# Expert weights in rows of four runs, and turns moved from TensorE to VectorE

## The chip, the cores and the metric

One NeuronCore of a Trainium2 chip runs the whole program. The time is the device time of one execution in microseconds (us). The engines are TensorE (PE in the profile, its weight loads PEld), VectorE (DVE), ScalarE (ACT), GpSimd (POOL) and SyncE (SP). SP issues all the transfers here, and the core has 16 DMA engines that carry them.

## The reference, cut to what matters

The program is a small network of two blocks over 256 context and 256 latent tokens of 1024 features, all in float32. The change touches two places of it. The first is a mixture of eight experts over the 256 latent tokens, of which each token uses two:

```python
D_MODEL = 1024
D_FF = 2816
N_EXPERTS = 8
TOP_K = 2

def _swiglu(h, w1, w3, w2):
    return (jax.nn.silu(h @ w1) * (h @ w3)) @ w2
```

`w1` and `w3` of an expert are 1024 x 2816 and `w2` is 2816 x 1024, so that an expert has 3 x 1024 x 2816 x 4 bytes = 34.6 MB of weights and the eight together have 276.8 MB. A token's outputs of its two experts are weighted by its gates and summed. The second place is an attention with two softmaxes per head, subtracted from each other, over four heads and 256 latent queries.

## The kernel before, in words

Every engine has its own instruction stream, and semaphores order them. The program runs through its stages one after the other; weights come through ring buffers in SBUF.

**The expert stage.** A router on the chip gives each expert the places of its tokens. Each of the eight experts is one block of work (more blocks would follow if an expert had more than 96 tokens). A block works on 96 token slots in three groups (`g`) of 32. The loop over blocks is the same on TensorE, VectorE, ScalarE and SP; `pe_moe`, `ve_moe` and `ac_moe` count each engine's steps in it.

- **Gather.** A selection matrix `pm` (tokens x slots, ones and zeros) picks the expert's tokens out of `atok`. TensorE multiplies it (`gather`, L1282), and ScalarE copies the result to `ac_` (L1868), with the features on the partitions. This is done for the next block while a block still runs.
- **Up.** The 2816 hidden features are cut into two halves `p` of 1408, and each half into four parts of 352. For a half, TensorE goes over eight feature tiles `k` of 128; for each it takes one item of `w1` and one of `w3`. A matmul has 32 slots of `ac_` as its stationary side and 352 columns of an item as its moving side, and four of them stand side by side in the array's columns and write four quarters of the partitions (L1337).
- **Gated values.** ScalarE takes silu of one product (L1889), VectorE multiplies it by the other into `hid` (L2638). A row of `hid` is a slot, and slots of part `t` lie on partitions 32t to 32t+31.
- **Turn.** The down product needs the hidden features on the partitions. TensorE turns `hid` in pieces of 128, 128 and 96 columns (`hidden_turned`, L1321), ScalarE copies the pieces to `gT` (L1894, L1895).
- **Down.** 24 items of `w2` follow, for each part two of 128 rows and one of 96; each takes 12 matmuls of 256 columns (L1359). The outputs are copied by ScalarE (L1904), and brought back to the tokens with the gates by `outputs_back` (L1293); VectorE adds them to `h` (L2611).

**Its transfers.** A block has 56 items (`ITEMS`): 32 of `w1` and `w3` (128 rows of 1408 numbers, 704 KB) and 24 of `w2` (512 or 384 KB). They go through 14 slots (`MRING`). SP issues item i when TensorE has used the item that was in its slot before (L584), so up to 14 items are under way or waiting. A source is 128 rows (or 96) that follow each other in the matrix, row on partition:

```python
src = src[one, k * P:k * P + P, n0:n0 + MCOLS]
...
src = src.rearrange("e p n -> p (e n)")
sy.dma_start(dst, src).then_inc(m_full[i % MRING], 16)
```

**The attention with two softmaxes** has eight units `w_`. For each, TensorE makes scores (`scores2`, L1453), VectorE finds the maxima (`maxima2`, L2685), ScalarE takes exponents, VectorE combines the two (L2693 to L2696), TensorE turns the weights (`weights_turned2`, its instructions are at L737), ScalarE copies them, and TensorE multiplies by the values (`values2`, L1472). Scores of unit w+1 are issued ahead of the turn of unit w. They use banks 0 and 1 or 2 and 3 in turn.

Of the kernel before, what the change touches and what calls it, by code (L numbers as in the profile page):

```python
# [21 lines left out]
ACT = mybir.ActivationFunctionType  # L22
# [224 lines left out]
def build(nc, w, out, counts, stop="end"):  # L247
# [5 lines left out]
    with ExitStack() as ctx:  # L253
# [169 lines left out]
        ac_ = cut(arena, 0, KT, CAP)  # L423
        hid = cut(arena, 768, 2, GROUPS_OF, PART)
        gT = cut(arena, 2880, 2, GROUPS_OF, 3 * P)
# [7 lines left out]
        TURN_BANKS = ((4, 5, 4), (4, 0, 1))  # L433
# [41 lines left out]
        def _(sy):  # L475
# [49 lines left out]
            while s < len(slots):  # L525
# [45 lines left out]
                if s == first["moe"]:  # L571
# [7 lines left out]
                    def block_in(e, expert):  # L579

                        one = bass.ds(expert, 1)
                        for i in range(ITEMS):
                            prev = (i - MRING) % ITEMS
# [12 lines left out]
                            src = src.rearrange("e p n -> p (e n)")  # L596
# [24 lines left out]
        def _(pe):  # L621
# [680 lines left out]
            def expert_block(e, mark):  # L1302
# [9 lines left out]

                def landed(i):
                    pe.wait_ge(m_full[i % MRING], e * (16 * (ITEMS // MRING)) + 16 * (i // MRING + 1))
                    return m_slots[i % MRING]

                def hidden_turned(p, g):

                    b = bank[TURN_BANKS[p][g]]
                    for o, n in PIECES:  # L1320
                        i = nc.tensor.transpose(b[0:n, o:o + P], hid[:, p, g, o:o + n], ident)  # L1321
                    i.then_inc(pe_moe, mark(PEM, ("turned", p, g)))

                for p in range(2):
                    for k in range(KT):
                        ws = [landed(16 * p + 2 * k + i) for i in range(2)]
                        for g in range(GROUPS_OF):
                            if k == 0 and p == 0 and g == 0:
                                of_act_last("gathered")
# [4 lines left out]
                            for i_ in range(2):  # L1334
                                b = bank[UP_BANKS[p][2 * g + i_]]
                                for t in range(4):
                                    i = mm(b[32 * t:32 * t + 32, 0:PART], ac_[:, k, 32 * g:32 * g + 32],  # L1337
# [12 lines left out]
                for n, (p, t, piece) in enumerate(BLOCKS_AT):  # L1350
                    o, rows_ = PIECES[piece]
                    ws = landed(32 + n)
                    for g in range(GROUPS_OF):
                        if n == 0:
                            of_vec(("hid", 1, 0))
                        if n % 12 == 0:
                            of_act(("gT", p, g))
                        for q in range(4):
                            i = mm(bank[Y_BANKS[g]][32 * q:32 * q + 32, 0:256],  # L1359
                                   gT[0:rows_, p, g, o + 32 * t:o + 32 * t + 32],  # L1360
                                   ws[0:rows_, 256 * q:256 * q + 256], start=(n == 0),
                                   stop=(n == len(BLOCKS_AT) - 1), skip_group_check=True)
                    i.then_inc(pe_moe, mark(PEM, ("down", n)))
                    if n in (1, 2, 3):
                        of_vec(("hid", 1, n - 1))
                        if n == 1:
                            of_act(("gT", 0, 2))
                        hidden_turned(1, n - 1)
                    if n == 7:
                        of_vec(("hid", 1, 2))  # L1370
                        of_act(("gT", 1, 2))
# [25 lines left out]
            pe.wait_ge(ac_moe, blocks * aper + aper)  # L1397
            outputs_back().then_inc(pe_done, did(PE, "back last"))
# [162 lines left out]
        def _(ac):  # L1561
# [303 lines left out]
            def gathered(name, inc, counter):  # L1865

                for h in range(2):
                    act(ac_[:, 4 * h:4 * h + 4, :], cut(bank[4 - 4 * h], 0, 4, CAP), ACT.Copy  # L1868
                        ).then_inc(inc, did(counter, name if h else (name, 0)))

            ac.wait_ge(pe_done, at(PE, "gather first"))
            gathered("gathered first", act_done, AC)
# [5 lines left out]
            with ac.Fori(0, blocks) as e:  # L1878
# [4 lines left out]
                for p in range(2):  # L1883
# [7 lines left out]
                    for g in range(GROUPS_OF):  # L1891
                        of_pe(("turned", p, g))
                        b = bank[TURN_BANKS[p][g]]
# [922 lines left out]
```

## Time and profile before

| | |
|---|---|
| median of 3 runs | 3294.95 us (3294.92 to 3304.92) |
| the profiled execution | 3293.41 us, span 3291.6 us |
| TensorE busy | 3116.3 us, 95% of the span |
| VectorE busy | 1283.0 us, 39% |
| ScalarE busy | 588.3 us, 18% |
| granted clock of TensorE, mean | 0.972 |
| expert stage, first to last of its up and down matmuls | 1657.6 to 2455.6 us |

Each matmul in float32 stands in the profile as two records. Busy time of TensorE counts its records' modelled spans; where it is busy without a gap, the starts of records tell how fast it goes. The DMA share is the mean busy share of the 16 DMA engines; it can read a little over 1.

### The profile page before, as it was taken

What the parts mean: (1) busy time and instruction counts of PE and PEld (TensorE: products, weight loads), DVE (VectorE), ACT (ScalarE), POOL (GpSimd) and SP (SyncE); (2) the same over time, 40 slices, a digit from 0 to 9 for tenths busy, and PEclk for the clock granted to TensorE, in tenths of its full rate; (3) what the DMA queues carried; (4) which work ended last, traced back from release to release, by engine and by line L of the source; (5) the groups of instructions that cost most, each with busy time, mean ns of one, the idle gap of its engine ahead of it and who ended that gap; (6) DMA issues with size and microseconds to landing.
All of it is one profiled execution on the core that took longest, in us unless ns stands there. A gap on an engine that the chain in (4) does not pass through costs nothing.

```text
span 3291.6 us, 52527 instructions
## 1 busy us (share of the span) xinstructions
PE 3116.3 (95%) x22488; PEld 2069.7 (63%) x22488; DVE 1283.0 (39%) x2836; ACT 588.3 (18%) x1314; POOL 0.2 (0%) x4
## 2 busy tenths in 40 slices
PE   7999899999999999999999999999999879988998
PEld 5454799997344443457745555445557568876887
DVE  1568666666799887503410101000112232122211
ACT  2114222222211111203310110010111220012000
POOL 0000000000000000000000000000000000000000
PEclk8999999999999999999999999999999889999999
DMA  7241001001577886330189999999984114531452
GB/s 264 75 154 51 1 1 40 1 1 39 189 239 243 245 248 187 123 99 25 70 317 362 357 339 337 343 362 367 349 231 130 51 52 141 153 115 51 133 148 64
DMA packets 351595, 551.15 MB, mean 167 GB/s; under 512 B 14512, under 2 KB 292400, under 8 KB 348048
## 3 DMA queue, kind: packets, MB, share of 16 engines
q1 hardware_dynamic: 351376, 547.89, 50.2%
q8 instruction: 178, 2.92, 0.4%
q14 instruction: 41, 0.34, 0.0%
HBM read 546.80 MB, written 1.05 MB: 166 GB/s over the span
## 4 chain that ended last, share of the span: by engine, by line
PE 89%; DVE 6%; ACT 2%; DMA 2%; issue 1%; SPq 0%; DVEq 0%; ACTq 0%
PE bank L666 15%; PE bank L1337 14%; PE bank L928 9%; PE bank L1130 8%; PE bank L1359 8%; PE bank L1517 7%; PE bank L1144 3%; PE bank L631 3%; PE bank L745 3%; PE bank L1171 2%; PE bank L1075 2%; DVE mix L2079 2%; PE bank L912 1%; PE bank L1282 1%; DMA arena<-in_ada_w 1%; PE bank L1426 1%
## 5 line engine op out<-in xcount | busy, mean ns | idle before, releaser
L666 PE MATMUL bank<-a,ring 128*128 128x256 f32 (+1 forms) x1792 | 454.8, 417 | 19.0 <-ACT a L1614 12.0
L666 PEld LDWEIGHTS bank<-a,ring 128*128 128x128 f32 x1792 | 344.9, 193 | 126.5 <-issue 74.5
L2079 DVE SCALAR_TENSOR_TENSOR mix<-arena,csil,mix 128x256 f32<-128x256 f32 x1008 | 402.0, 476 | 45.6 <-ACT mix L1618 45.6
L1337 PE MATMUL bank<-ring,arena 128*32 128x352 f32 x5376 | 406.9, 461 | 2.7 <-ACT small L1876 2.7
L1337 PEld LDWEIGHTS bank<-ring,arena 128*32 128x32 f32 x5376 | 175.1, 110 | 221.4 <-issue 220.4
L1130 PE MATMUL bank<-a,ring 128*128 128x512 f32 x704 | 307.5, 596 | 6.8 <-ACT a L1614 6.8
L1130 PEld LDWEIGHTS bank<-a,ring 128*128 128x128 f32 x704 | 133.2, 191 | 179.7 <-issue 178.0
L1517 PE MATMUL bank<-arena,ring 128*128 128x256 f32 x1024 | 223.5, 379 | 1.9 <-DVE arena L2736 1.9
L1618 ACT ACTIVATE arena<-bank 128x256 f32<-128x256 f32 (+1 forms) x303 | 142.0, 473 | 451.7 <-PE bank L928 199.2
L2638 DVE TENSOR_TENSOR arena<-arena,bank 128x352 f32<-128x352 f32 x48 | 25.0, 521 | 501.3 <-ACT arena L1889 501.3
L1359 PE MATMUL bank<-ring,arena 128*32 128x256 f32 (+1 forms) x3840 | 219.0, 380 | 0.6 <-issue 0.6
L1517 PEld LDWEIGHTS bank<-arena,ring 128*128 128x128 f32 x1024 | 194.4, 190 | 29.1 <-DVE arena L2736 2.8
L928 PE MATMUL bank<-arena 128*128 128x128 f32 x1408 | 180.6, 281 | 3.1 <-DVE arena L2344 2.1
L928 PEld LDWEIGHTS bank<-arena 128*128 128x128 f32 x1408 | 166.4, 193 | 14.6 <-ACT arena L1618 6.7
L1359 PEld LDWEIGHTS bank<-ring,arena 128*32 128x32 f32 (+1 forms) x3840 | 121.9, 110 | 83.5 <-issue 9.5
L1144 PE MATMUL bank<-arena,ring 128*128 128x512 f32 x352 | 154.1, 597 | 2.1 <-DVE arena L2460 2.1
L2717 DVE TENSOR_SCALAR tmpA<-bank,mods 128x256 f32<-128x256 f32 x32 | 15.5, 484 | 288.4 <-PE bank L1517 213.9
L1144 PEld LDWEIGHTS bank<-arena,ring 128*128 128x128 f32 x352 | 67.5, 192 | 88.4 <-issue 85.5
L1567 ACT ACTIVATE mix<-a 128x256 f32<-128x256 f32 x64 | 21.8, 417 | 534.1 <-DVE a L1994 534.1
L1618 ACT ACTIVATE mix<-arena,csil 128x256 f32<-128x256 f32 x144 | 64.7, 499 | 261.6 <-DMA arena<-in_ada_w 160.6
L745 PE MATMUL bank<-a,ring 128*128 128x512 f32 (+1 forms) x224 | 99.1, 596 | 0.0
L2732 DVE TENSOR_SCALAR tmpA<-bank 128x256 f32<-128x256 f32 x64 | 27.2, 424 | 167.1 <-PE bank L666 167.1
(411 smaller groups left out, 3360.6 us busy)
## 6 DMA issues: line engine op xcount, KB each, us to landing
ring<-in_moe_w SPq DMA_DIRECT2D x224, 704.0 KB, 8.4
ring<-in_mlp_w SPq DMA_DIRECT2D x64, 1024.0 KB, 5.5
ring<-in_moe_w SPq DMA_DIRECT2D x112, 512.0 KB, 8.4
arena<-in_ada_w SPq DMA_DIRECT2D x96, 512.0 KB, 3.8
arena<-in_w_ada SPq DMA_DIRECT2D x48, 512.0 KB, 3.6
ring<-in_ffn_w SPq DMA_DIRECT2D x22, 1024.0 KB, 8.5
arena<-in_moe_w SPq DMA_DIRECT2D x32, 704.0 KB, 8.8
ring<-in_moe_w SPq DMA_DIRECT2D x48, 384.0 KB, 8.4
```

Of the source, the lines that this page charges most:

```text
L631: i = mm(bank[b][:, 0:tile.shape[-1]], const("mean"), tile, start=(k == 0), stop=(k == KT - 1))
L666: i = mm(bank[b][:, 0:n], ws[:, k, t * P:t * P + P], rhs[:, k, sl], start=(k == 0), stop=(k == KT - 1))
L745: i = mm(bank[RKV_BANK[n]][0:m, :], ws[:, k, n % 2 * P:n % 2 * P + m], aT[:, k, :], start=(k == 0), stop=(k == KT - 1), skip_group_check=True)
L928: i = mm(bank[b][:, o + P * m:o + P * m + P], lhs[:, m, :], rhs[:, m, :], start=True, stop=True, skip_group_check=True)
L1075: i = mm(bank[MIX_BANKS[j % 5]], ws[:, k, j % 2 * P:j % 2 * P + P], src, start=(k == 4), stop=(k == 3), skip_group_check=True)
L1130: i = mm(bank[2 * t + i_], ws[:, k, t * P:t * P + P], aT[:, k, :], start=(k == 0), stop=(k == KT - 1))
L1144: i = mm(bank[2 + n % 4], ws[:, k, :], G[:, k, :], start=(k == 0), stop=(k == FT - 1))
L1337: i = mm(b[32 * t:32 * t + 32, 0:PART], ac_[:, k, 32 * g:32 * g + 32], ws[i_][:, PART * t:PART * t + PART], start=(k == 0), stop=(k == KT ...
L1359: i = mm(bank[Y_BANKS[g]][32 * q:32 * q + 32, 0:256], gT[0:rows_, p, g, o + 32 * t:o + 32 * t + 32], ws[0:rows_, 256 * q:256 * q + 256], s ...
L1517: j = mm(bank[4 + n % 2][:, 0:TL], ws[:, k, :], G2[:, 16 * half + k, :], start=(half + k == 0), stop=(half * k == 15))
L1618: act(dst, src, ACT.Copy, scale=scale).then_inc(act_done, did(AC, name))
L2079: ins = V.scalar_tensor_tensor(dst, x, cond, dst, ALU.mult, ALU.add)
```

## The change

It has three parts.

1. **Rows of the weight items.** An item is now made of four runs of 32 rows. For `w1` and `w3` run t begins at row 256t + 32k; for `w2` at row 352t + 32c of the half (`DOWN`, c from 0 to 10). `w2` has 22 items of 128 rows, a block has 54 items. The constants `PIECES`, `BLOCKS_AT` and `TURN_BANKS` go.
2. **Turns.** `gather` now has 32 columns of the selection as its stationary side in four column tiles and 256 columns of tokens as its moving side. VectorE's 32 x 32 block transpose turns its result from PSUM into `ac_` (3 per block, 128 x 256), and turns each `hid` into `gT` in SBUF (6 per block, 128 x 352). TensorE's `hidden_turned` and ScalarE's copies of both go.
3. **Scores.** `scores2` runs two units ahead in place of one.

```diff
-PIECES = ((0, 128), (128, 128), (256, 96))
-BLOCKS_AT = [(p, t, i) for p in range(2) for t in range(4) for i in range(3)]
-ITEMS = 32 + len(BLOCKS_AT)
+DOWN = [(p, c) for p in range(2) for c in range(PART // 32)]
+ITEMS = 32 + len(DOWN)
...
                             if i < 32:
                                 k, n0 = i % 16 // 2, MCOLS * (i // 16)
-                                src = w["moe_w3" if i % 2 else "moe_w1"][0]
-                                src = src[one, k * P:k * P + P, n0:n0 + MCOLS]
+                                src = w["moe_w3" if i % 2 else "moe_w1"][0][one, :, n0:n0 + MCOLS]
+                                src = src.rearrange("e (t r) n -> (e t) r n", t=4)[:, 32 * k:32 * k + 32, :]
                             else:
-                                p, t, piece = BLOCKS_AT[i - 32]
-                                o, n = PIECES[piece]
-                                f0 = MCOLS * p + PART * t + o
-                                src = w["moe_w2"][0][one, f0:f0 + n, :]
-                                dst = dst[0:n, 0:D]
-                            src = src.rearrange("e p n -> p (e n)")
+                                p, c = DOWN[i - 32]
+                                src = w["moe_w2"][0][one, MCOLS * p:MCOLS * p + MCOLS, :]
+                                src = src.rearrange("e (t r) n -> (e t) r n", t=4)[:, 32 * c:32 * c + 32, :]
+                                dst = dst[:, 0:D]
                             sy.dma_start(dst, src).then_inc(m_full[i % MRING], 16)
...
-                for f in range(KT):
+                for g in range(GROUPS_OF):
                     for c in range(2):
-                        i = mm(bank[0 if f >= 4 else 4][:, (f % 4) * CAP:(f % 4) * CAP + CAP],
-                               atok[:, c, f * P:f * P + P], pm[:, c, :], start=(c == 0), stop=(c == 1),
-                               skip_group_check=True)
+                        for q in range(4):
+                            i = mm(bank[4 * (g // 2)][32 * q:32 * q + 32, 256 * (g % 2):256 * (g % 2) + 256],
+                                   pm[:, c, 32 * g:32 * g + 32], atok[:, c, 256 * q:256 * q + 256],
+                                   start=(c == 0), stop=(c == 1), skip_group_check=True)
...
                             if k == 0 and p == 0 and g == 0:
-                                of_act_last("gathered")
+                                of_vec_last(("gathered", GROUPS_OF - 1))
+                                of_act_last("gates")
...
-                        if p == 1 and k in (2, 3, 4):
-                            if k == 2:
-                                of_vec(("hid", 0, 2))
-                            if k == 4:
-                                of_act(("gT", 0, 0))
-                            hidden_turned(0, k - 2)
...
-                        if n == 0:
+                        if n == 0 and g == 0:
+                            of_vec(("gT", 0, 2))
                             of_vec(("hid", 1, 0))
-                        if n % 12 == 0:
-                            of_act(("gT", p, g))
+                        if c == 0 and p == 1:
+                            of_vec(("gT", 1, g))
...
             scores2(0)
+            scores2(1)
             for w_ in range(len(DIFF_UNITS)):
-                if w_ + 1 < len(DIFF_UNITS):
-                    scores2(w_ + 1)
+                if w_ + 2 < len(DIFF_UNITS):
+                    scores2(w_ + 2)
                 weights_turned2(w_)
...
+            def gathered(g, inc, counter, name):
+                V.transpose(ac_[:, g, :], bank[4 * (g // 2)][:, 256 * (g % 2):256 * (g % 2) + 256]
+                            ).then_inc(inc, did(counter, (name, g)))
...
+                def hidden_turned(p, g):
+
+                    ve.wait_ge(ve_moe, e * per + at(VEM, ("hid", p, g)))
+                    V.transpose(gT[:, p, g, :], hid[:, p, g, :]).then_inc(ve_moe, did(VEM, ("gT", p, g)))
```

**SP, the transfers of `w2` in a block.** The last two numbers or three are the shape of the side in SBUF. Before, at the start of the down items:

```order
L597 DMA ring<-in_moe_w 128x1024
L597 DMA ring<-in_moe_w 96x1024
L597 DMA ring<-in_moe_w 128x1024
L597 DMA ring<-in_moe_w 128x1024
L597 DMA arena<-in_moe_w 96x1024
```

and in the changed kernel:

```order
L598 DMA ring<-in_moe_w 128x1x1024
L598 DMA ring<-in_moe_w 128x1x1024
L598 DMA ring<-in_moe_w 128x1x1024
L598 DMA ring<-in_moe_w 128x1x1024
L598 DMA arena<-in_moe_w 128x1x1024
```

The 96-row transfers are gone, and each side has three dimensions now: 128 x 1 x 1024 in SBUF against 4 x 32 x 1024 in the source, as the slicing in the diff leaves it. The transfers of `w1` and `w3` change from 128x1408 to 128x1x1408 (source 4 x 32 x 1408) in the same way.

**TensorE, the second half of a block.** Before (here one row stands for both records of a matmul), from the middle of the second up half to the end of the down product:

```order
L1337 MATMUL bank<-arena 32x352 x24
L1337 MATMUL bank<-ring,arena 32x352 x48
L1359 MATMUL bank<-ring,arena 32x256 x24
L1321 MATMUL bank<-consts,arena 128x128 x2
L1321 MATMUL bank<-consts,arena 96x128
L1359 MATMUL bank<-ring,arena 32x256 x12
L1321 MATMUL bank<-consts,arena 128x128 x2
L1321 MATMUL bank<-consts,arena 96x128
L1359 MATMUL bank<-ring,arena 32x256 x12
```

and now, up to the next block's up product (L1336 is the up product, L1352 the down product, L1284 the gather):

```order
L1336 MATMUL bank<-ring,arena 32x352 x48
L1352 MATMUL bank<-ring,arena 32x256 x96
L1295 MATMUL bank<-arena 128x256 x24
L1352 MATMUL bank<-arena 32x256 x24
L1352 MATMUL bank<-ring,arena 32x256 x60
L1366 MATMUL bank<-consts,arena 128x128 x6
L1352 MATMUL bank<-ring,arena 32x256 x24
L1284 MATMUL bank<-arena 32x256 x24
L1352 MATMUL bank<-ring,arena 32x256 x60
```

The turns between the products are gone, the gather has 24 matmuls of 256 columns in place of 16 of 96, and the down product has 264 matmuls in place of 288.

**TensorE, the attention with two softmaxes.** Before, its first units:

```order
L1453 MATMUL bank<-arena 128x512 x4
L737 MATMUL bank<-consts,arena 128x128 x4
L1453 MATMUL bank<-arena 128x512 x2
L737 MATMUL bank<-consts,arena 128x128 x4
L1472 MATMUL bank<-arena 128x128 x4
L1453 MATMUL bank<-arena 128x512 x2
```

and now:

```order
L1441 MATMUL bank<-arena 128x512 x6
L738 MATMUL bank<-consts,arena 128x128 x4
L1441 MATMUL bank<-arena 128x512 x2
L738 MATMUL bank<-consts,arena 128x128 x4
L1460 MATMUL bank<-arena 128x128 x4
L1441 MATMUL bank<-arena 128x512 x2
```

The order around each unit is the same, but the scores that stand ahead of a turn are those of one unit later.

## Rows read from the trace of the kernel before

**Rows 1.** The page of the profile: the span and the engines' busy time.
```profile
span 3291.6 us, 52527 instructions
PE 3116.3 (95%) x22488; PEld 2069.7 (63%) x22488; DVE 1283.0 (39%) x2836; ACT 588.3 (18%) x1314; POOL 0.2 (0%) x4
```

**Rows 2.** Waits, 1650 to 2470 us: who waited for whom, total, times, longest.
```profile
PE bank L1337 <- ACT small L1876: 2.7, 1, 2.7
...
PE bank L1359 <- issue: 0.6, 1, 0.6
```

**Rows 3.** Waits of SP's queue in the same stretch.
```profile
SPq L597 <- PE bank L1337: 351.8, 128, 22.3
SPq L597 <- PE bank L1359: 196.3, 172, 4.6
```

**Rows 4.** Windows: the third expert's block as a whole.
```profile
core 0: us, PE busy (x) PEld busy (x) DVE busy (x) ACT busy (x) POOL busy (x), PEclk, DMA share, GB/s
1857.92:1957.28 99.36, 99.36 (x1452) 51.33 (x1448) 8.40 (x22) 10.02 (x26) 0.00 (x0) 1.00 1.01 352
```

**Rows 5.** Timeline of TensorE in the second block: start, us, instructions.
```profile
1758.56 21.49 PE L1337 MATMUL bank<-ring,arena 128*32 128x352 f32 x288
...
1797.73 0.55 PE L1321 MATMUL bank<-consts,arena 128*128 128x128 f32 x3
1798.21 3.76 PE L1337 MATMUL bank<-ring,arena 128*32 128x352 f32 x48
...
1845.09 3.81 PE L1282 MATMUL bank<-arena 128*128 128x96 f32 x32
1848.83 6.69 PE L1359 MATMUL bank<-ring,arena 96*32 96x256 f32 x120
1855.33 2.77 PE L1359 MATMUL bank<-arena 128*32 128x256 f32 x48
```

**Rows 6.** Windows of the second block, while `w1` and `w3` load.
```profile
1763.00:1770.00 7.00, 7.00 (x100) 3.14 (x96) 0.00 (x0) 0.00 (x0) 0.00 (x0) 1.00 1.01 418
1770.00:1780.00 10.00, 10.00 (x140) 4.45 (x136) 0.00 (x0) 0.00 (x0) 0.00 (x0) 1.00 1.02 414
1790.00:1800.00 10.00, 10.00 (x135) 4.30 (x131) 0.00 (x0) 0.54 (x2) 0.00 (x0) 1.00 1.02 409
```

**Rows 7.** Windows of the last block, while `w2` loads.
```profile
2398.70:2406.70 8.00, 8.00 (x107) 3.43 (x111) 0.00 (x0) 1.09 (x4) 0.00 (x0) 1.00 1.02 229
...
2414.70:2422.70 8.00, 8.00 (x131) 4.29 (x125) 0.09 (x1) 1.63 (x6) 0.00 (x0) 1.00 1.04 250
2422.70:2430.70 8.00, 8.00 (x148) 5.29 (x141) 1.99 (x6) 0.00 (x0) 0.00 (x0) 1.00 1.03 267
```

**Rows 8.** Timeline of SP: the first expert items issued.
```profile
1630.48 6.42 SPq L597 DMA_DIRECT2D ring<-in_moe_w  x12
```

**Rows 9.** The page's transfers by line: count, KB each, median us to landing.
```profile
ring<-in_moe_w SPq DMA_DIRECT2D x224, 704.0 KB, 8.4
```

**Rows 10.** The chain that ended last: the last down matmuls.
```profile
2446.32 9.26 PE bank L1359 x168
```

**Rows 11.** Timeline of TensorE in the attention with two softmaxes, one unit.
```profile
2610.40 1.12 PE L737 MATMUL bank<-consts,arena 128*128 128x128 f32 x4 [2.50 <-DVE arena L2696]
2611.31 1.92 PE L1472 MATMUL bank<-arena 128*128 128x128 f32 x8
2613.16 1.13 PE L1453 MATMUL bank<-arena 64*128 64x512 f32 x4
2616.79 1.11 PE L737 MATMUL bank<-consts,arena 128*128 128x128 f32 x4 [2.51 <-DVE arena L2696]
```

**Rows 12.** Timeline of VectorE in the same unit.
```profile
2614.34 1.29 DVE L2685 TENSOR_REDUCE small<-bank 128x1 f32<-128x512 f32 x2 [3.99 <-PE bank L1453]
...
2615.99 0.75 DVE L2696 SCALAR_TENSOR_TENSOR arena<-arena,small 128x512 f32<-128x512 f32 x1
```

**Rows 13.** Groups of instructions in the third block: the nearest VectorE row.
```profile
L2638 DVE TENSOR_TENSOR arena<-arena,bank 128x352 f32<-128x352 f32 x6 | 3.1, 521 | 63.7 <-ACT arena L1889 63.7
```

More of the change, by code:

```diff
@@ L53, with uses @@
 MRING, MCOLS, PART = 14, 1408, 352
-PIECES = ((0, 128), (128, 128), (256, 96))
-BLOCKS_AT = [(p, t, i) for p in range(2) for t in range(4) for i in range(3)]
-ITEMS = 32 + len(BLOCKS_AT)
+DOWN = [(p, c) for p in range(2) for c in range(PART // 32)]
+ITEMS = 32 + len(DOWN)
+def uses(i):
+    return len(range(i % MRING, ITEMS, MRING))
 RING = 6
@@ L420, in build @@
         NA_UNITS = [(j, qt) for j in range(KT) for qt in range(2)]
-        ac_ = cut(arena, 0, KT, CAP)
+        ac_ = cut(arena, 0, GROUPS_OF, 256)
         hid = cut(arena, 768, 2, GROUPS_OF, PART)
-        gT = cut(arena, 2880, 2, GROUPS_OF, 3 * P)
+        gT = cut(arena, 2880, 2, GROUPS_OF, PART)
         yp, pgt = cut(arena, 5184, GROUPS_OF, 256), cut(arena, 5952, GROUPS_OF, 256)
@@ L582, in block_in @@
                         for i in range(ITEMS):
-                            prev = (i - MRING) % ITEMS
+                            prev = i - MRING if i >= MRING else i + MRING * (uses(i) - 1)
                             sy.wait_ge(pe_moe, e * per + (at(PEM, taken(prev)) - (per if i < MRING else 0)))
@@ L1311, in of_vec, with of_vec_last @@
                     pe.wait_ge(ve_moe, e * vper + at(VEM, name))
+                def of_vec_last(name):
+                    pe.wait_ge(ve_moe, e * vper + (at(VEM, name) - vper))
                 def landed(i):
-                    pe.wait_ge(m_full[i % MRING], e * (16 * (ITEMS // MRING)) + 16 * (i // MRING + 1))
+                    pe.wait_ge(m_full[i % MRING], e * (16 * uses(i)) + 16 * (i // MRING + 1))
                     return m_slots[i % MRING]
[L1317 to L1322, printed above, removed]
                 for p in range(2):
@@ L1343, in expert_block @@
                             i.then_inc(pe_moe, mark(PEM, ("up", p, k)))
[L1344 to L1351 removed]
+                for n, (p, c) in enumerate(DOWN):
                     ws = landed(32 + n)
                     for g in range(GROUPS_OF):
[L1354 removed]
+                        if n == 0 and g == 0:
+                            of_vec(("gT", 0, 2))
                             of_vec(("hid", 1, 0))
[L1356 to L1357 removed]
+                        if c == 0 and p == 1:
+                            of_vec(("gT", 1, g))
                         for q in range(4):
                             i = mm(bank[Y_BANKS[g]][32 * q:32 * q + 32, 0:256],
[L1360 to L1362 removed]
+                                   gT[:, p, g, 32 * c:32 * c + 32],
+                                   ws[:, 256 * q:256 * q + 256], start=(n == 0),
+                                   stop=(n == len(DOWN) - 1), skip_group_check=True)
                     i.then_inc(pe_moe, mark(PEM, ("down", n)))
[L1364 to L1368, printed above, removed]
                     if n == 7:
                         of_vec(("hid", 1, 2))
[L1371 removed]
                         of_act_last(("y", 2))
@@ L1397, in _ @@
             pe.wait_ge(ac_moe, blocks * aper + aper)
+            pe.wait_ge(ve_moe, blocks * vper + vper)
             outputs_back().then_inc(pe_done, did(PE, "back last"))
@@ L1863, in _ @@
             pper, vper = at(PEM, ("per", "moe")), at(VEM, ("per", "moe"))
[L1865 to L1872, printed above, removed]
             ac.wait_ge(act_done, now(AC))
@@ L1890, in _ @@
                             ).then_inc(ac_moe, did(ACM, ("sg", p, g)))
-                    for g in range(GROUPS_OF):
-                        of_pe(("turned", p, g))
-                        b = bank[TURN_BANKS[p][g]]
-                        act(gT[:, p, g, 0:256], b[:, 0:256], ACT.Copy).then_inc(ac_moe, did(ACM, ("gT part", p, g)))
-                        act(gT[0:96, p, g, 256:384], b[0:96, 256:384], ACT.Copy
-                            ).then_inc(ac_moe, did(ACM, ("gT", p, g)))
                 of_pe("gates turned")
@@ L1899, in _ @@
                 act(pgt[:, 2, :], bank[2][:, 0:256], ACT.Copy).then_inc(ac_moe, did(ACM, "gates"))
-                of_pe("gather")
-                gathered("gathered", ac_moe, ACM)
-                of_pe(("down", len(BLOCKS_AT) - 1))
+                of_pe(("down", len(DOWN) - 1))
                 for g in range(GROUPS_OF):
@@ L2604, in _ @@
             pper, aper = at(PEM, ("per", "moe")), at(ACM, ("per", "moe"))
+            def gathered(g, inc, counter, name):
+                V.transpose(ac_[:, g, :], bank[4 * (g // 2)][:, 256 * (g % 2):256 * (g % 2) + 256]
+                            ).then_inc(inc, did(counter, (name, g)))
             ve.wait_ge(pe_done, at(PE, "gather first"))
+            for g in range(GROUPS_OF):
+                gathered(g, vec_done, VE, "gathered first")
+            ve.wait_ge(vec_done, now(VE))
             counts.count[VEM] = per
@@ L2640, in _ @@
                                         ).then_inc(ve_moe, did(VEM, ("hid", p, g)))
+                        if g:
+                            hidden_turned(p, g - 1)
+                    hidden_turned(p, GROUPS_OF - 1)
                 of_pe("back")
@@ L2643, in _ @@
                     back_added(f, ve_moe, VEM, "h")
+                of_pe("gather")
+                for g in range(GROUPS_OF):
+                    gathered(g, ve_moe, VEM, "gathered")
                 ve.wait_ge(ve_moe, e * per + now(VEM))
```

3 lines of the change are left out of this document (1 added, 2 removed).

## The prediction

> **What bounds the kernel now.** I read the page first: TensorE is busy for 95% of the span [rows 1], so the question for every stage is whether TensorE is what ends it. For the expert stage the windows answer it. A block takes 99.36 us and TensorE is busy for all of them, at the full clock of 1.00, which is 2.4 GHz [rows 4]. In the list of waits TensorE waited in the whole stage once for ScalarE, 2.7 us, and never for a transfer [rows 2]; SP, on the other hand, waited for TensorE 128 and 172 times, 351.8 and 196.3 us [rows 3]. So TensorE bounds the stage, and the transfers follow it.
>
> The reader is to see in the same row that the margin behind it is thin: 34.6 MB in 99.36 us are 348 GB/s, the row shows 352, and the 16 DMA engines' share reads 1.01 [rows 4]. While `w1` and `w3` load, at a share of 1.01 to 1.02, they move 409 to 418 GB/s [rows 6]; I take 415, which is 26 GB/s for each of the 16 engines. While `w2` loads in the last block the share is as full (1.02 to 1.04), but they move only 229 to 267 [rows 7], about 244, or 15.3 GB/s for each. A row of an item is some kilobytes long in both (5.6 and 4.1); what differs is that a third of the `w2` items have 96 rows. How the rows of an item are dealt to the engines thus decides the rate. That is the point at which this change must be judged.
>
> **What it takes from TensorE.** Per block:
> - six turns go. One takes from 1797.73 to 1798.21 [rows 5], 0.48 us: 2.88 us.
> - 24 down items become 22. A record goes by every 54.2 ns (1848.83 to 1855.33 for 120) [rows 5], an item has 12 matmuls or 24 records: 48 records are 2.60 us.
> - the gather takes from 1845.09 to 1848.83 now [rows 5], 3.74 us. Its 24 new matmuls have the shape of the down product, so 48 x 54.2 ns = 2.60 us: 1.14 us less.
>
> That is 6.62 us of 99.36, and 53 us over eight blocks, if TensorE stays the bound.
>
> **What VectorE gets.** Nine transposes per block that the trace of before does not show. The nearest row is the gating product of the same 128 x 352, 0.52 us [rows 13]. From nothing to four times that, one costs 0 to 2.1 us; I take 0.5, and 4.5 us per block beside 8.40 busy of 99 [rows 4]. What waits for them: the up product of the next block waits for the last gathered turn, which may start when the gather ends and has five down items of 1.30 us = 6.5 us of cover, and three turns fit even at 2.1 us. The down product's second half waits for the second half's turns with eleven items of cover, 14 us. So they cost nothing in the block; if the cover were gone they would cost up to 6 us per block. Ahead of the first block the three turns stand on the way once: +1.5 us, against some 1 us that the first gather saves. ScalarE's copies that go were not waited for.
>
> **The attention.** A unit takes from 2610.40 to 2616.79 [rows 11], 6.4 us, and TensorE waits 2.5 us of it for VectorE's combined weights; VectorE in turn waited 3.99 us for the scores [rows 12]. With scores two units ahead, the maxima (1.29) and the combination (about 1.1 with its two small instructions) follow each other without TensorE between, 2.4 us per unit, and TensorE's own work of 1.12 + 1.92 + 1.13 = about 4.1 us becomes the bound. Seven periods shrink by some 2.3 us: -16 us. If the order of waits gives nothing: 0.
>
> **What it does to the transfers.** An item's source was 128 rows in one dimension, and is now 4 runs of 32 rows; its side in SBUF is still 128 rows. Packets keep their length. What may change is the dealing. In the trace of before every large transfer has 128 or 96 rows as its outermost dimension on both sides, and the share shows that all 16 engines work. If an item is dealt by the outermost dimension, 4 on the one side and 128 on the other leave four equal portions, and four engines carry everything while twelve stand idle.
>
> The Trainium skill, "DMA: Bandwidth & Descriptors", section "Why a DMA increments its semaphore by 16 and not by 1", states just this: the number of engines is the largest up to 16 that divides the slowest dimension of both access patterns, and the lowest-numbered ones are taken. By that rule this item runs on four. No row of before can show it, as none has such a shape.
>
> I take four engines as the likeliest case. The price: 276.8 MB at 4 x 26 = 104 GB/s are 2662 us; at 4 x 15.3 = 61 GB/s 4538 us. Four runs of 32 neighbouring rows are less even over SBUF than a 128-row item dealt over sixteen engines, but whole, so I stay near the upper rate and take 25 GB/s per engine, 100 in all: 2768 us, or 346 us per block. TensorE's work in a block, 92.7 us, lies beside that, even at the lower of its clocks (185 us).
>
> **The sum.** The first item is issued at 1630.48 [rows 8] and moves 1 us later: 1631.5. The last lands 2768 + 2 us later; TensorE's last down item is 1.3 us: 4402.8. Before, the last down matmul ended at 2446.32 + 9.26 = 2455.58 [rows 10], and 3291.6 - 2455.58 = 836.0 us of span followed it [rows 1, 10]; less 16 for the attention: 5222.8. Around the span lay 3293.41 - 3291.6 = 1.8 us, and the median of the runs lies 1.5 us over the profiled one: **5226 us**, 1.59 times before. I say 5230.
>
> **The rivals.**
> - **Four engines that get in each other's way (31%).** Engines now walk partitions 0, 32, 64 and 96 upwards together, and if two of them need one entry to SBUF at a time, they share its rate. For it: the 244 GB/s at a full share [rows 7], which show that a dealing can cost 40% of the rate. Against: a delay of one engine by some rows takes the pair apart for good. At 61 GB/s: 4538 - 2768 = 1770 us more, 7000 us; with only `w2` so, 1845 + 1513 = 3358 us, 5820. It decides when the rate falls below 93 GB/s, 5430 us. The Trainium skill, "SBUF — State Buffer", section "Door 1: The DMA port swizzle", says that partitions 32 apart lie on one port, so that engines one and two, and three and four, would meet; if they always did, each pair would have one engine's rate, 52 GB/s in all by the rate of the rows, and the time would be 7780.
> - **All sixteen engines as before (12%).** Then the stage stays TensorE's: 3295 - 53 - 16 = 3226 us, faster by 2%. It ends on the other side, and it decides if the dealing goes by rows in SBUF (128, unchanged) or if an item is cut anew on its way. For it: the side in SBUF is unchanged, packets too, and an average of 34.6 MB in 92.7 us is 373 GB/s, below the 415 of [rows 6]. Against: the two sides have to be cut in step, and nothing in the profile shows a cut within an outer dimension.
> - **Eight engines, or another cut (2%):** 208 GB/s, 1331 us, about 3790.
>
> **How the numbers follow.** Four engines near their full rate have 55%; their own range is 5100 (104 GB/s gives 5120) to 5450 (93 GB/s). With the second case, which reaches to 7000 and lies mostly below 6500, the range is 5050 to 6850; outside it are the sixteen engines, the other cuts and the far end of the second case, together some 18%. A measurement of this kernel tells a difference of 0.3%, 10 us. Slower: 55 + 31 + 2 = 88%; faster: 11%; within 0.3% if sixteen engines carry the items but collide in the way of [rows 7]: 1%.
>
> **What the new profile would show.** Right: in the expert stage a DMA share of about 0.25 at 95 to 104 GB/s, and a block of 335 to 365 us; landing 80 to 100 us after issue in place of 8.4 [rows 9], as 14 items queue before four engines; TensorE waiting for transfers at its up and down products for some 70% of the stage. The transposes would read 0.4 to 0.6 us. In the attention a unit would take 4 to 4.5 us. Collisions would show as the same share of 0.25 with 60 to 90 GB/s. Wrong: a share near 1 in the stage, blocks of 93 us, landing near 8 us.

## The result, and the profile after

| | before | changed |
|---|---|---|
| median | 3294.93 us (3294.56 to 3304.92) | 5072.97 us (5070.70 to 5079.43) |
| ratio | 1 | 1.5388, 95% interval 1.5356 to 1.5421 |
| span of the profiled execution | 3291.6 us | 5077.6 us |
| TensorE busy | 95% of the span | 69% |
| a block of the expert stage | 99.36 us | 326.05 us |

The change makes the kernel 1.54 times as slow. The page of the changed kernel, its head, its 40 slices, and the groups that answer to the up and down products (busy us, mean ns, then idle time before them and what ended it):

```profile
span 5077.6 us, 51698 instructions
PE 3500.5 (69%) x22104; PEld 2121.0 (42%) x22104; DVE 1314.6 (26%) x2911; ACT 553.7 (11%) x1200; POOL 0.2 (0%) x4
...
DMA  5300003778420222222222222222222223235243
GB/s 192 127 33 1 26 10 112 232 236 236 151 85 12 106 106 106 106 106 106 106 106 107 106 106 106 106 107 106 106 107 106 107 106 129 77 109 149 74 133 91
...
L1336 PE MATMUL bank<-ring,arena 128*32 128x352 f32 x5376 | 643.5, 650 | 889.5 <-DMA ring<-in_moe_w 817.3
...
L1352 PE MATMUL bank<-ring,arena 128*32 128x256 f32 x3840 | 364.0, 533 | 379.9 <-DMA ring<-in_moe_w 379.9
```

Half of the span is now twenty equal slices of the expert stage, all at 106 GB/s and a DMA share of two tenths. Before, the up product had waited once, 2.7 us [rows 2]; now it waits 817.3 us for transfers into the ring, and the down product 379.9. One whole block by windows, from one up product to the next, answers to [rows 4]:

```profile
2007.75:2333.80 326.05, 158.44 (x1398) 61.88 (x1398) 12.19 (x31) 5.88 (x12) 0.00 (x0) 0.66 0.26 106
```

The reader is to see three numbers in it. The DMA share fell from 1.01 to 0.26, which is four of 16 engines (0.25) and a little reading over. The rate fell from 352 to 106 GB/s, and 34.6 MB in 326.05 us are the same 106. And the granted clock fell from 1.00 to 0.66: TensorE pauses half of the time, and its records last longer for it (650 ns in place of 461 for an up matmul's record), which costs nothing here, as the transfers end last. The Trainium skill, "DMA: Bandwidth & Descriptors", "Why a DMA increments its semaphore by 16 and not by 1", says that a transfer runs on the largest number of engines up to 16 that divides both slowest dimensions; the share of this row agrees with four.

TensorE's timeline shows the rhythm, one step of the up product for each pair of items:

```profile
2021.35 6.34 PE L1336 MATMUL bank<-ring,arena 128*32 128x352 f32 x48 [7.28 <-DMA ring<-in_moe_w]
2034.95 6.37 PE L1336 MATMUL bank<-ring,arena 128*32 128x352 f32 x48 [7.25 <-DMA ring<-in_moe_w]
2048.54 6.40 PE L1336 MATMUL bank<-ring,arena 128*32 128x352 f32 x48 [7.22 <-DMA ring<-in_moe_w]
```

A step comes every 13.6 us: 2 x 0.721 MB in 13.6 us are 106 GB/s, 26.5 for each of four engines, slightly more than the 26 that each of sixteen reached before [rows 6].

In the attention with two softmaxes the part that was to help did help. TensorE's timeline there, against [rows 11]:

```profile
4417.89 0.66 PE L738 MATMUL bank<-consts,arena 128*128 128x128 f32 x4
4418.38 1.06 PE L1460 MATMUL bank<-arena 128*128 128x128 f32 x8
4419.37 1.13 PE L1441 MATMUL bank<-arena 64*128 64x512 f32 x4
4420.46 0.66 PE L738 MATMUL bank<-consts,arena 128*128 128x128 f32 x4
```

A unit takes 2.57 us (4417.89 to 4420.46) in place of 6.4, with no wait in it.

### The profile page after: what moved, and what is told of

The parts are those of the page before. It is cut to its first block, busy times and chain, and to the rows that moved or that the text cites. A ratio compares the mean times of both kernels' runs of the same rounds, so it can differ in the third digit from the quotient of the medians.

```text
span 5077.6 us, 51698 instructions
## 1 busy us (share of the span) xinstructions
PE 3500.5 (69%) x22104; PEld 2121.0 (42%) x22104; DVE 1314.6 (26%) x2911; ACT 553.7 (11%) x1200; POOL 0.2 (0%) x4
## 3 DMA queue, kind: packets, MB, share of 16 engines
q8 instruction: 175, 2.87, 0.2%
HBM read 546.80 MB, written 1.05 MB: 108 GB/s over the span
## 4 chain that ended last, share of the span: by engine, by line
PE 45%; SPq 25%; DMA 23%; DVE 4%; issue 1%; ACT 1%; DVEq 0%; ACTq 0%
SPq L598 25%; DMA ring<-in_moe_w 17%; PE bank L667 10%; PE bank L929 6%; PE bank L1131 5%; DMA arena<-in_moe_w 5%; PE bank L1506 4%; PE bank L1336 3%; PE bank L1145 2%; PE bank L632 2%; PE bank L746 2%; PE bank L1172 1%; DVE mix L2052 1%; PE bank L1076 1%; PE bank L913 1%
## 5 line engine op out<-in xcount | busy, mean ns | idle before, releaser
L1336 PE MATMUL bank<-ring,arena 128*32 128x352 f32 x5376 | 643.5, 650 | 889.5 <-DMA ring<-in_moe_w 817.3
L1336 PEld LDWEIGHTS bank<-ring,arena 128*32 128x32 f32 x5376 | 241.2, 150 | 1292.9 <-issue 1292.9
L1352 PE MATMUL bank<-ring,arena 128*32 128x256 f32 x3840 | 364.0, 533 | 379.9 <-DMA ring<-in_moe_w 379.9
L1352 PEld LDWEIGHTS bank<-ring,arena 128*32 128x32 f32 x3840 | 139.7, 141 | 592.8 <-DMA ring<-in_moe_w 479.5
L1870 ACT ACTIVATE arena<-bank 128x352 f32<-128x352 f32 x48 | 22.3, 464 | 1711.0 <-PE bank L1336 1711.0
L1336 PE MATMUL bank<-arena 128*32 128x352 f32 x768 | 90.6, 642 | 127.4 <-DMA arena<-in_moe_w 127.4
L2592 DVE SCALAR_TENSOR_TENSOR h<-bank,mods,h 128x256 f32<-128x256 f32 x72 | 29.0, 476 | 332.7 <-PE bank L1295 332.7
L1336 PEld LDWEIGHTS bank<-arena 128*32 128x32 f32 x768 | 34.0, 148 | 184.0 <-issue 184.0
```

The lines of the kernel that those rows point to most:

```text
L1336: i = mm(b[32 * t:32 * t + 32, 0:PART], ac_[:, g, 32 * k:32 * k + 32], ws[i_][:, PART * t:PART * t + PART], start=(k == 0), stop=(k == KT ...
L1352: i = mm(bank[Y_BANKS[g]][32 * q:32 * q + 32, 0:256], gT[:, p, g, 32 * c:32 * c + 32], ws[:, 256 * q:256 * q + 256], start=(n == 0), stop= ...
```

## The experiments

The theory is that the shape of an item's source, 4 x 32 rows, puts it on four engines. The rivals are that rows scattered in HBM are slow to read, that VectorE's turns or the new waits hold the blocks up, and that engines get in each other's way.

**Everything but the rows (e1_columns).** The items are 128 rows that follow each other again, and the pairing of features is kept by the columns that TensorE's tiles take.

```diff
-                                src = w["moe_w3" if i % 2 else "moe_w1"][0][one, :, n0:n0 + MCOLS]
-                                src = src.rearrange("e (t r) n -> (e t) r n", t=4)[:, 32 * k:32 * k + 32, :]
+                                src = w["moe_w3" if i % 2 else "moe_w1"][0]
+                                src = src[one, k * P:k * P + P, n0:n0 + MCOLS].rearrange("e p n -> p (e n)")
...
-                                src = w["moe_w2"][0][one, MCOLS * p:MCOLS * p + MCOLS, :]
-                                src = src.rearrange("e (t r) n -> (e t) r n", t=4)[:, 32 * c:32 * c + 32, :]
+                                f0 = MCOLS * p + P * c
+                                src = w["moe_w2"][0][one, f0:f0 + P, :].rearrange("e p n -> p (e n)")
...
-                                   pm[:, c, 32 * g:32 * g + 32], atok[:, c, 256 * q:256 * q + 256],
+                                   pm[:, c, 32 * g:32 * g + 32],
+                                   atok[:, c, :].rearrange("p (k q j) -> p k q j", q=4, j=32)[:, :, q, :],
...
-                                           ws[i_][:, PART * t:PART * t + PART], start=(k == 0),
+                                           ws[i_].rearrange("p (c t j) -> p c t j", t=4, j=32)[:, :, t, :], start=(k == 0),
```

> All of the change is kept but the rows of the items: each item is again 128 rows that follow each other, one outermost dimension on both sides. TensorE's column tiles take columns in runs of 32 in their place, so that the pairing of features stays right and the output is the reference's. Theory (an item is dealt over as many engines as its outermost dimensions share, here four of 16): the DMA share goes back to near 1, TensorE bounds the stage again, a block takes 92.7 us and the time is 3295 - 53 (turns, gather, two down items) - 23 (attention, as the profile after shows it) = 3219 us, 3210 to 3235. Rival (the turns on VectorE or the new waits hold the blocks up): it stays near 5070. Rival (a moving side in runs of 32 columns is slower): more than 3235.

Measured: 3212.14 us against 3294.67, ratio 0.9749 (0.9733 to 0.9766). Its second and third block by windows:

```profile
1754.42:1846.18 91.76, 91.76 (x1402) 46.57 (x1398) 12.19 (x31) 5.87 (x12) 0.00 (x0) 1.00 0.97 381
1846.18:1937.94 91.76, 91.76 (x1402) 46.39 (x1398) 12.18 (x31) 5.87 (x12) 0.00 (x0) 1.00 0.97 379
```

TensorE is busy without a gap at the full clock, and the block is 7.6 us shorter than in [rows 4]. The time is within the expected 3210 to 3235 us. The way in which an item takes its rows is thus the whole loss, and the rest of the change is a gain of 2.5%. VectorE does as many and as long instructions as in the changed kernel (12.19 us), so its turns are no cause. Runs of 32 columns cost TensorE nothing: 48 records of the up product take 3.56 us here (1775.72 to 1779.28) and 3.55 before (1779.87 to 1783.42). This version beats both kernels.

**Eight runs of 16 rows,** in the changed kernel.

```diff
-                                src = src.rearrange("e (t r) n -> (e t) r n", t=4)[:, 32 * k:32 * k + 32, :]
+                                src = src.rearrange("e (t r) n -> (e t) r n", t=8)[:, 16 * k:16 * k + 16, :]
...
-                                src = src.rearrange("e (t r) n -> (e t) r n", t=4)[:, 32 * c:32 * c + 32, :]
+                                src = src.rearrange("e (t r) n -> (e t) r n", t=8)[:, 16 * c:16 * c + 16, :]
```

> The changed kernel with items of eight runs of 16 rows in place of four of 32 (features are then paired with the wrong weights; the work is the same). Theory (number of engines = what divides both outermost dimensions, 8 and 128): eight engines at 26.5 GB/s are 212 GB/s, 276.8 MB take 1306 us, the time is 1635 + 1306 + 3 + 816 + 2 = 3762 us, DMA share 0.5. Rival (rows scattered in HBM are slow to read): with twice as many runs the rate stays at 106 GB/s or falls, 5070 us or more. Rival (partitions that share an entry): a rate below 212 at a share of 0.5.

Measured: 3815 us, once. In the first of these windows the share is 0.51 and the rate 209 GB/s:

```profile
1700.00:2300.00 600.00, 405.17 (x5024) 186.06 (x5028) 43.08 (x108) 19.87 (x41) 0.00 (x0) 0.89 0.51 209
2300.00:2900.00 600.00, 386.13 (x4818) 179.21 (x4806) 42.62 (x110) 21.21 (x43) 0.00 (x0) 0.91 0.51 203
```

More scattered rows, twice the rate: the scatter is not the cause, the number of runs is what counts. The rate falls 1 to 4% short of 212, and the time is 53 us over the expected 3762.

**Sixteen runs of 8 rows,** the same edit with `t=16` and 8.

> The same with sixteen runs of 8 rows (features paired with the wrong weights again). Theory: 16 divides both sides, so all 16 engines carry an item; if they reach 373 GB/s or more, TensorE bounds the stage and the time is 3219 us, with a DMA share near 1. The rows of an engine are then 8 neighbouring partitions, and if engines 32 partitions apart hold each other up as the mixed items of the down product did before (244 GB/s), 276.8 MB take 1134 us and the time is 3590. Rival (scattered rows): 5070 us or more.

Measured: 3469 us, once.

```profile
1700.00:2000.00 300.00, 236.01 (x3312) 121.71 (x3304) 27.27 (x68) 13.13 (x27) 0.00 (x0) 0.97 1.02 277
2000.00:2300.00 300.00, 241.09 (x3474) 127.54 (x3474) 30.76 (x81) 14.84 (x30) 0.00 (x0) 0.98 1.02 285
```

All 16 engines are busy (1.02), so the theory's count holds again, but they move 277 and 285 GB/s, not 373: the stage is bound by transfers, between the two cases of the expectation. Here is a second effect, which four engines did not have. Both the way to SBUF and the scatter in HBM differ from e1_columns here, so this run alone does not say which of them it is.

**The same rows as four transfers,** 32 rows each, 32 outermost on both sides, in the changed kernel.

```diff
-                            sy.dma_start(dst, src).then_inc(m_full[i % MRING], 16)
+                            for t in range(4):
+                                sy.dma_start(dst[32 * t:32 * t + 32, :], src[t:t + 1, :, :].rearrange("t r n -> (t r) n")
+                                             ).then_inc(m_full[i % MRING], 16)
...
-                    pe.wait_ge(m_full[i % MRING], e * (16 * uses(i)) + 16 * (i // MRING + 1))
+                    pe.wait_ge(m_full[i % MRING], e * (64 * uses(i)) + 64 * (i // MRING + 1))
```

> The changed kernel with the same rows, but each item as four transfers of 32 rows, one for each run, 32 outermost on both sides; the output is the reference's. Theory: each transfer is dealt over 16 engines, 2 rows each, so the share goes back to near 1 with the very same rows in the same places: 3219 us if TensorE bounds the stage, up to 3600 if the dealing in pairs of rows reaches only 244 GB/s. SP issues 216 transfers per block in place of 54; at 0.33 us they are 71 us, below a block's 92.7. Rival (scattered rows): 5070 us.

Measured: 3621 us, once.

```profile
1700.00:2740.00 1040.00, 764.00 (x9962) 368.52 (x9966) 85.31 (x217) 41.14 (x84) 0.00 (x0) 0.93 1.02 241
```

The very rows of the changed kernel, in the same places, at 241 GB/s and a full share in place of 106 and 0.26. With this nothing is left of the rival of scattered rows as the reason for 106. The time is 21 us over the 3600 that the expectation gave as its upper case. That the rate stays at 241 looks like the second effect again, but these transfers also have a quarter of the size, and no run took the two apart.

**Only `w1` and `w3` in four runs,** in the kernel before.

```diff
-                                src = src[one, k * P:k * P + P, n0:n0 + MCOLS]
+                                src = src[one, :, n0:n0 + MCOLS]
+                                src = src.rearrange("e (t r) n -> (e t) r n", t=4)[:, 32 * k:32 * k + 32, :]
...
-                            src = src.rearrange("e p n -> p (e n)")
+                            if i >= 32:
+                                src = src.rearrange("e p n -> p (e n)")
```

> The kernel before with the items of w1 and w3 alone in four runs of 32 rows, w2 as before (features are paired with the wrong weights in the up product; the work is the same). Theory: the four engines that carry w1 and w3 also carry a sixteenth each of w2: 5.77 + 0.72 = 6.49 MB per block and engine, at 26.5 GB/s 245 us per block, 1959 in all, 4435 us; if w2 can't run beside w1 and w3 it takes 1741 + 378 us and ends at 4595. Rival (the down product's rows were what cost): near 3400.

Measured: 4577 us, once, near the second case (4595) and far from the rival's 3400: `w1` and `w3` in four runs are enough for most of the loss, and the `w2` items hardly run beside them. Two stretches of a block, with `w2` under way and without:

```profile
1840.00:1880.00 40.00, 21.42 (x257) 10.04 (x261) 1.56 (x3) 3.02 (x9) 0.00 (x0) 0.72 0.78 223
...
1920.00:1960.00 40.00, 17.36 (x144) 6.52 (x144) 0.00 (x0) 0.00 (x0) 0.00 (x0) 0.70 0.26 106
```

TensorE still does its turns and ScalarE its copies here, as before the change, and the stage is as slow as its transfers make it: VectorE's turns are not needed for the loss either. The up product's steps come every 13.6 us where `w1` and `w3` load alone, as in the changed kernel; where `w2` loads too, two of them come 15.7 and 20.7 us apart (1827.21, 1842.90, 1863.63).

**VectorE's turns six times over,** in e1_columns.

```diff
-                    V.transpose(gT[:, p, g, :], hid[:, p, g, :]).then_inc(ve_moe, did(VEM, ("gT", p, g)))
+                    for again in range(6):
+                        V.transpose(gT[:, p, g, :], hid[:, p, g, :]).then_inc(
+                            ve_moe, did(VEM, ("gT", p, g) if again == 5 else ("gT again", p, g, again)))
+                        if again < 5:
+                            ve.wait_ge(ve_moe, e * per + at(VEM, ("gT again", p, g, again)))
```

> e1_columns with each of VectorE's turns of the gated values done six times over, one after the other (output unchanged): 30 more per block, at 0.53 us and a wait each some 18 us more of VectorE's time per block. Theory (the turns lie under the products): the same time as e1_columns, 3212 us within 0.2%. Rival (VectorE's turns are on the path of the block): up to 144 us more, 3356.

Measured: 3214.81 us (3212.61 to 3215.34) against 3212.14 for e1_columns, 0.08% more, while the ratio to before is 0.9752 (0.9736 to 0.9769) and 0.9749. The group of the turns in a stretch of one block's length:

```profile
L2609 DVE STREAM_TRANSPOSE arena<-arena 128x352 f32<-128x352 f32 x36 | 19.4, 542 | 1.0
```

In the changed kernel six turns took 3.0 us of a block. 16 us more of VectorE's time per block cost nothing that can be measured: the turns inside the blocks are covered with much to spare.

**Scores two units ahead alone,** in the kernel before.

```diff
             scores2(0)
+            scores2(1)
             for w_ in range(len(DIFF_UNITS)):
-                if w_ + 1 < len(DIFF_UNITS):
-                    scores2(w_ + 1)
+                if w_ + 2 < len(DIFF_UNITS):
+                    scores2(w_ + 2)
```

> The kernel before with one part of the change alone: scores two units ahead. Theory: the attention's stretch of matmuls falls from 49.0 us to the 26.1 us that it takes in the changed kernel, since both the waits for VectorE go and TensorE, now without pauses, is granted a higher clock (0.74 there before, 0.92 after): 3294.7 - 22.9 = 3272 us, 3268 to 3276. Rival (only the waits go, as the prediction had it): 3279 us.

Measured: 3272.62 us (3267.24 to 3274.43) against 3294.98, ratio 0.9927 (0.9911 to 0.9944): 22 us, as expected, and the whole interval lies on the side of a gain; the runs (3267 to 3274 us) stay clear of the rival's 3279. Before, TensorE's waits for the combined weights were, between 2595 and 2655 us (total, times, longest):

```profile
PE bank L737 <- DVE arena L2696: 18.6, 7, 3.5
```

The stretch shrinks by 22.9 us, more than these waits were long, and 1.8 us of waits for VectorE are still left in it. The clock in the attention, before and in this version (windows of 36 and 26 us):

```profile
2610.00:2646.00 36.00, 23.06 (x93) 17.17 (x94) 13.05 (x29) 12.79 (x38) 0.00 (x0) 0.74 0.00 1
```

```profile
2600.00:2626.00 26.00, 22.12 (x126) 13.89 (x123) 19.07 (x44) 19.20 (x59) 0.00 (x0) 0.93 0.13 40
```

**`w2` in whole items of 128 rows,** in the kernel before. It asks for the reason of [rows 7].

```diff
-                                f0 = MCOLS * p + PART * t + o
+                                f0 = MCOLS * p + PART * t + o - (P - n)
+                                n = P
```

> The kernel before with each 96-row item of w2 read as 128 rows, from 32 rows further up (the third piece of each part is then paired with the wrong weights; 4.2 MB more per block). It asks what held the transfers at 244 GB/s beside a full share in the last block. Theory (items of 96 rows are dealt 6 neighbouring rows to an engine, and engines meet at the same partitions' entries): with whole items only, the rate where w2 loads is no longer tied to a full share; where TensorE lets SP run ahead it comes to 380 to 415 GB/s, and landing stays below 10 us. Rival (rows of 4 KB are slow as such): 230 to 290 GB/s at a share of 1 again, landing 11 to 16 us in the last block. The time stays 3295 us either way, as TensorE bounds the stage.

Measured: 3295.71 us, once, the same time. The windows of [rows 7], the stretch from 2400 to 2425 us, and the issues in it:

```profile
2414.70:2422.70 8.00, 8.00 (x125) 4.15 (x121) 1.04 (x2) 2.02 (x6) 0.00 (x0) 1.00 0.95 335
2422.70:2430.70 8.00, 8.00 (x144) 5.29 (x144) 0.00 (x0) 0.54 (x2) 0.00 (x0) 1.00 0.99 365
...
2400.00:2425.00 25.00, 25.00 (x355) 11.89 (x351) 1.57 (x3) 4.11 (x13) 0.00 (x0) 1.00 0.88 305
...
ring<-in_moe_w SPq DMA_DIRECT2D x13, 512.0 KB, 5.3
```

In the kernel before the same 25 us read

```profile
2400.00:2425.00 25.00, 25.00 (x368) 12.21 (x364) 1.57 (x3) 3.57 (x11) 0.00 (x0) 1.00 1.02 240
...
ring<-in_moe_w SPq DMA_DIRECT2D x9, 512.0 KB, 12.8
ring<-in_moe_w SPq DMA_DIRECT2D x5, 384.0 KB, 15.3
```

With whole items the same rows of 4 KB land after 5.3 us in place of 12.8, and the 25 us move 305 GB/s at a share of 0.88 in place of 240 at 1.02. The first two windows of [rows 7] read 314 and 256 GB/s, at shares of 0.87 and 0.79, in place of 229 and 230. So the items of 96 rows were most of what made the transfers slow. They were not all of it: divided by the share, the four windows give 324 to 369 GB/s, where `w1` and `w3` give about 406 (414 at 1.02). The rate of 380 was not reached in any of them, in part because the engines had pauses (SP waited for TensorE), in part for a reason that stays open; the length of the row is not excluded for that part.

## Why the prediction was right, point by point

- **The bound and its margin.** Right, and the step that decided it was to ask how an item's rows are dealt to the engines. Dealing by the outermost dimensions of both sides gave the number, four, and the rate of w1 and w3 [rows 6] divided by 16 gave the price of one engine; the runs with four, eight and sixteen runs of rows show shares of 0.26, 0.51 and 1.02.
- **The rate of an engine.** Mis-sized. I took 25 GB/s for each, between the 26 of [rows 6] and the 15.3 of [rows 7]; it measured 26.5. From 1 us after the first issue (1635.3) to the last landing at 4258.5 the stage's transfers took 2623 us, where the sum has 2768 + 2: 147 us less. The upper row alone was the right one; that four runs are "less even over SBUF" had no row behind it and cost most of the miss.
- **The range.** 5073 lies inside 5050 to 6850, but below 5100, the lower end that I gave the case of four engines by itself: I had put its rate at 104 GB/s at most, and it was 106. The case was right by its mechanism, and its own range was too narrow on the fast side; the lower end of the whole range held by 23 us.
- **Four engines in each other's way.** This did not happen: four engines that start 32 partitions apart run at full rate. The rule of the port map (the Trainium skill, "SBUF — State Buffer", "Door 1: The DMA port swizzle") would have engines one and two meet on one port; the row of the changed kernel, 26.5 GB/s each, shows no such loss. With all 16 engines busy a loss is there, though: 277 to 285 GB/s with sixteen runs of 8 rows (by the theory each engine then has 8 neighbouring partitions), 241 with transfers of 32 rows (2 of each quarter), 244 where a third of the items has 96 rows [rows 7], and 409 to 418 with whole items of 128 rows of `w1` and `w3`. The 96-row items are shown to be most of the loss in [rows 7]. That the dealing is what the slow cases share is argued; which partitions an engine had is in no view, and whether shared ports are the reason is not shown.
- **TensorE's gain.** 7.6 us per block against 6.62 worked out (e1_columns). The turns (2.87), the gather (1.15) and the two items came as worked out; 1.0 us more comes from the products themselves, 0.42 in the up product and 0.56 in the down product. Most of it is a cost of the turns that I left out: before, a stretch of product records that ends at a turn takes longer. 48 records took 3.55 us without a turn behind them (1779.87 to 1783.42) and 3.69 with one (1798.21 to 1801.90):

```profile
1779.87 3.73 PE L1337 MATMUL bank<-arena 128*32 128x352 f32 x48
1783.42 14.38 PE L1337 MATMUL bank<-ring,arena 128*32 128x352 f32 x192
...
1798.21 3.76 PE L1337 MATMUL bank<-ring,arena 128*32 128x352 f32 x48
1801.90 0.55 PE L1321 MATMUL bank<-consts,arena 128*128 128x128 f32 x3
```

  At the six turns of that block this is 0.11 to 0.14 us each, 0.76 in all.
- **VectorE's turns.** 0.53 us for 128 x 352 and 0.42 for 128 x 256 against 0.5 taken; inside a block they are covered, as the sixfold run shows. At the start of the stage they are not: from VectorE's last step of the router's arithmetic to the first up matmul it is 0.62 us before (1657.01 to 1657.63) and 1.76 in e1_columns (1658.20 to 1659.96), so the three turns cost 1.1 us there against 1.5 foreseen. The shorter gather, 5.35 us in place of 6.36, gave nothing back, as VectorE's arithmetic ended after it in both.
- **The attention.** 22.9 us where 16 were worked out. The mechanism was right, the waits went; but the period went to 2.57 us and not to 4.1. The step that was mis-sized is "TensorE's own work of 1.12 + 1.92 + 1.13": its first two terms were durations at a lowered clock (0.74 in that stretch), and they are 0.66 and 1.06 where the waits are gone and 0.93 is granted. The third stayed 1.13.
- **The profile foretold.** The share (0.26 for 0.25) and the turns came as said. The rate (106 for 95 to 104 GB/s) and the block (326.05 for 335 to 365 us) lay outside on the fast side. TensorE waited for 51% of the block of 326.05 us, not 70%: its work was counted at the full clock, and at 0.66 its records filled 158.44 us of it.
- **Landing.** I wrote that an item would land 80 to 100 us after its issue, as 14 queue. This failed: the last item was issued at 4235.66 and landed 22.8 us later, the one landing of an expert item that the profile gives here. SP's issue took the time instead, below.
- **The sum.** 5226 holds 1.5 us from the profiled execution to the median, so it says 5224.5 for the profiled one. Less 147 (rate), less 7 (attention), plus 3.8 (the first issue came at 1634.3), plus 1.5 (the last down item at a low clock), plus about 3 in what follows the stage (816.3 us, where 836.0 less 22.9 would be 813.1; 0.9 of it comes before the attention, 2.3 behind it, for a reason that stays open) is 5079; the profiled execution took 5079.4. The median lay 6.5 us below it and not 1.5 above.

## What to carry to other kernels

Before a transfer's rows are rearranged, look at the outermost dimension of both sides: here 4, 8 and 16 runs of rows gave a quarter, a half and all of the engines, and 1.54, 1.16 and 1.05 times the time of before (the last two from one run each). Where a new layout is wanted, let the compute side take strided columns and leave each transfer as 128 rows that follow each other: that kept the right features paired, at no cost to TensorE, and the kernel gained 2.5% in place of losing 54%. And where TensorE pauses, look at the granted clock before its durations are added up: in the attention, closing 18.6 us of waits gained 22.9.

## What the runs showed that I had not expected

- **SP's issue blocks.** An issue of an item takes 0.33 us before and in e1_columns, and 6.3 us in the changed kernel, nearly the time that the item itself takes at 106 GB/s (6.8 us). The groups of SP's queue (ns, least, median, most) in the changed kernel, and with eight runs:

```profile
L598 SPq DMA_DIRECT2D ring<-in_moe_w x384: 532/6334/14481, 1634.3 to 4235.7; - x192
```

```profile
L598 SPq DMA_DIRECT2D ring<-in_moe_w x384: 599/2939/8779, 1631.6 to 2981.3; - x192
```

  So some four items were ahead of the engines and not 14 (22.8 us to landing, at 5.0 us for each `w2` item at the end of the stage), and a wait of SP is seen as a long issue and not as a wait. It is not the waiting of transfers as such that does it. With the same rows as four transfers the stage is bound by its transfers too and a transfer of `w1` or `w3` lands after 17.0 us, but the issues stay short:

```profile
L599 SPq DMA_DIRECT2D ring<-in_moe_w x1536: 315/316/1648, 1634.1 to 2787.7; - x192
```

  With sixteen runs the median is 1.26 us. An estimate from rates and landings, if rows are dealt evenly over the engines, of the rows that wait before each engine: about 150 in the changed kernel (4.6 items of 32 rows), 86 with sixteen runs (about 281 GB/s for the 27.6 us that an item of `w1` or `w3` takes to land there between 1700 and 2300 us, 8 rows of each item) and 45 with four transfers (241 GB/s for 17.0 us, 2 rows of each). Issues grow long in this order, so a limit on what waits before one engine would fit; no run tested it. A deeper ring of buffers would probably add nothing in the changed kernel, as its four engines never paused (the share is 0.26 from 1680 to 4200 us); this was not run either.
- **Shares near 1 don't mean a full rate.** At a share of 1.02 the engines moved 241 GB/s (the same rows as four transfers), 277 (sixteen runs) and 414 (`w1` and `w3` before).
